# The cache stage of a decoder step in pairs of steps, with part of its transposes moved to VectorE

## The chip, the cores and the metric

One Trainium2 chip, one core of it. The time is that of one execution on the device, in microseconds (us). A core has TensorE (PE, matrix products and transposes), VectorE (DVE), ScalarE (ACT), GpSimd (POOL) and SyncE (SP, here only DMA). Each runs its own list of instructions in order, and they wait for each other by semaphores.

## The reference

One inference step of a decoder layer that has two head groups (a gated delta rule and latent attention) and an MLP, for a prompt of 528 tokens (16 of them meta tokens) and for 8 sample sequences with 4 new tokens each. The part that matters here is the attention of the samples over their past, 4096 keys per sequence. A key is a latent of 256 numbers and a rotary part of 32, and the latent is also the value:

```python
def latent_scores(q_lat, q_pe, c, k_pe):
    s = jnp.einsum('bqhc,bkc->bhqk', q_lat, c) + jnp.einsum('bqhr,bkr->bhqk', q_pe, k_pe)
    return s.astype(jnp.float32) * MLA_SCALE

def sample_attention(q_lat, q_pe, c_new, kpe_new, c_past, kpe_past):
    ...
    p = jax.nn.softmax(jnp.concatenate([s_past, s_new], axis=-1), axis=-1).astype(c_new.dtype)
    return jnp.einsum('bhqk,bkc->bqhc', p[..., :P], c_past) + jnp.einsum('bhqk,bkc->bqhc', p[..., P:], c_new)
```

The past lies in pages of 128 keys, in an order that a page table gives. There are 8 heads, so a sequence has 32 query rows (8 heads by 4 tokens). All of it is fp32.

## The kernel before

The stages follow each other on PE: projections, the gated delta rule, queries and keys, the prompt's attention, then the **cache stage**, then the output product and the MLP (`big_product` and `weight_tile`, lines 589 to 591 of the profile), whose weights SP loads in 1 MB pieces (`load_weights`, L420) and ACT and DVE split into a high and a low part (L1222, L1721).

The cache stage has 16 steps, n = 0 to 15. Steps 0 to 7 belong to sequences 0 to 3 (g = 0), steps 8 to 15 to sequences 4 to 7. In a step each of four sequences b takes 512 keys. POOL fetches them by four indirect DMAs (`gather`, L2328) into `CN[n % 4][b]`, which holds 128 partitions by 4 keys by 288 numbers; there are four such sets. POOL also packs the rotary parts of the four sequences together (`pack_rope`, `KRN`).

The scores need the keys with their 288 numbers along the partitions, so PE transposes them, nine tiles of four 128x128 blocks a step: tiles 0 to 3 the first 128 latents of each sequence, 4 to 7 the other 128, tile 8 the packed rotary parts (`cache_transposes`, L1078). They go into four PSUM banks in turn, and DVE (tiles 0, 2, 4, 6, L2166) and ACT (the others, L1636) copy them to `CT[0]` to `CT[8]`. The score products (`cache_scores`, L1089) give each sequence 32 rows of the output, so four of them lie beside each other on 32 columns of PE each; the rope product (`cache_rope_scores`, L1096) takes all four at once with a query matrix that is zero off its blocks. A step's scores fill one bank, 3 or 4 in turn.

Then comes one softmax step: `cache_max` (L2171 to L2174) reduces 512 scores per row on DVE, takes the running maximum (`ML`) and the difference, `cache_exp` (L1643, L1644) takes the exponential on ACT into `PE_`, `cache_p` (L1104) transposes P on PE, ACT copies it to `PTE` (L1657), `cache_values` (L1113) multiplies it by the latents as they lie in `CN`, and `accumulate` (L2179, L2180) scales and adds on DVE.

The order is written out by hand. On PE, step n's nine transposes are interleaved with the second half of step n-1's scores, the values of step n-2, the first half of step n's scores and P of step n-1, so that what a product needs was issued well ahead of it. ACT and DVE have the same loop. A gather of step n+1 waits for the values of step n-3 (`ce_pv`), since it fills the same buffers.

The stage starts when the prompt's last output is copied (`po_copied`). After it DVE scales the sums (L2193, L2194), PE forms the samples' outputs (L1136, L1143), and the output product starts. Gathers 0 and 1 are made before the stage; 2 and 3 when the prompt's last value product (`pv_done`) is through.

Of the kernel before, what the change touches and what calls it, by code (L numbers as in the profile page):

```python
# [127 lines left out]
def build(nc, big_at, row_at, a):  # L128
# [160 lines left out]
    KRN, PE_, PTE = [], [], []  # L289
    at = r4  # L290
    for i in range(2):
        for name, held, shape in (("KRN", KRN, [P, 4, 4, DR]), ("PE", PE_, [P, 512]), ("PTE", PTE, [P, 4, P])):
            t, at = put(f"{name}{i}", shape, F32, at)
            held.append(t)
    ACC, at = put("ACC", [P, 2, KV], F32, at)
    SME, at = put("SME", [P, 2, 4], F32, at)
# [3 lines left out]
    QF, at = put("QF", [P, 2, 2, P], F32, spec_at)  # L300
    QRF, at = put("QRF", [P, 2, P], F32, at)
    assert at <= r4
    rows_of = 4 * (KV + DR) * 4
    cn_at = [[x + rows_of * b for b in range(4)] for x in (w_at, w_at + 4 * rows_of, x_at + 4 * rows_of, r1)]
# [3 lines left out]
    CT, at = [None] * 9, x_at  # L308
    for i in range(9):
        CT[i], at = put(f"CT{i}", [P, 512], F32, at)  # L310
# [3 lines left out]
    CT_BANKS = (0, 1, 2, 7)  # L314
    CT_DVE = {0: 1, 2: 2, 4: 3, 6: 4}
    CT_ACT = {1: 1, 3: 2, 5: 3, 7: 4, 8: 5}
# [19 lines left out]
    with ctx:  # L336
# [38 lines left out]
        def wait_copied(eng, n, u):  # L375

            if u in CT_DVE:
                eng.wait_ge(sem("ct_dve"), 4 * n + CT_DVE[u])
            else:
                eng.wait_ge(sem("ct_act"), 5 * n + CT_ACT[u])  # L380

        def wait_scored(eng, n, u):

            if n >= 0:
                eng.wait_ge(sem("ct_used"), 3 * n + (1 if u < 4 else 2 if u < 8 else 3))
# [22 lines left out]
        def _(sp):  # L408
# [90 lines left out]
        def _(pe):  # L499
# [444 lines left out]
            def new_transposes(g):  # L944
                pe.wait_ge(sem("new_exp"), g + 1)
                if g:
                    pe.wait_ge(sem("new_acc"), 1)
                pe.transpose(PS[0:NS, 6, 0:P], PE_[0][:, 0:NS], ident).then_inc(sem("new_pt"), 1)

            def new_values(g):  # L950
                pe.wait_ge(sem("new_ptc"), g + 1)
                pe.matmul(PS[:, 6, 0:KV], PTE[0][0:NS, 0, :], CNEW[:, :], start=True, stop=True)                  .then_inc(sem("new_pv"), 1)
# [112 lines left out]
            pe.wait_ge(sem("po_copied"), NT_)  # L1065

            def cache_transposes(n, u):

                x = 9 * n + u
                if x >= 4:  # L1070
                    wait_copied(pe, (x - 4) // 9, (x - 4) % 9)
                if u == 8:
                    pe.wait_ge(sem("kr_packed"), n + 1)
                elif u == 0:
                    pe.wait_ge(sem(f"cn_in{n % 4}"), 64 * (n // 4 + 1))
                for j in range(4):
                    src = CN[n % 4][u % 4][:, j, P * (u // 4):P * (u // 4) + P] if u < 8 else KRN[n % 2][:, j, :, :]
                    last = pe.transpose(PS[:, CT_BANKS[x % 4], P * j:P * j + P], src, ident)  # L1078
                last.then_inc(sem("ct_mm"), 1)

            def cache_scores(n, c):

                if c == 0 and n >= 2:
                    pe.wait_ge(sem("ce_exp"), n - 1)
                g, bank = n // 8, 3 + n % 2
                for b in range(4):
                    wait_copied(pe, n, 4 * c + b)
                for b in range(4):
                    last = pe.matmul(PS[32 * b:32 * b + 32, bank, :], QF[:, g, c, 32 * b:32 * b + 32], CT[4 * c + b][:, :],  # L1089
                                     start=(c == 0), stop=False)  # L1090
                last.then_inc(sem("ct_used"), 1)

            def cache_rope_scores(n):

                wait_copied(pe, n, 8)
                pe.matmul(PS[:, 3 + n % 2, :], QRF[:, n // 8, :], CT[8][:, :], start=False,  # L1096
                          stop=True).then_inc(sem("ct_used"), 1)

            def cache_p(n):
                pe.wait_ge(sem("ce_exp"), n + 1)  # L1100
                if n >= 1:
                    pe.wait_ge(sem("ce_ptc"), n)
                for j in range(4):
                    last = pe.transpose(PS[:, 5, P * j:P * j + P], PE_[n % 2][:, P * j:P * j + P], ident)  # L1104
                last.then_inc(sem("ce_pt"), 1)

            def cache_values(n):
                pe.wait_ge(sem("ce_ptc"), n + 1)
                if n >= 1:
                    pe.wait_ge(sem("acc_done"), n)  # L1110
                for j in range(4):
                    for b in range(4):
                        last = pe.matmul(PS[32 * b:32 * b + 32, 6, 0:KV], PTE[n % 2][:, j, 32 * b:32 * b + 32],  # L1113
                                         CN[n % 4][b][:, j, 0:KV], start=(j == 0), stop=(j == 3))
                last.then_inc(sem("ce_pv"), 1)

            for n in range(18):
                for u in range(9):
                    if n < 16:
                        cache_transposes(n, u)  # L1120
                    if 1 <= n <= 16 and u == 1:
# [1306 lines left out]
```

## Time and profile before

| | |
|---|---|
| Median of 3 runs | 1035.58 us (1034.27 to 1035.91) |
| The profiled execution | 1032.82 us |
| Its span, first to last instruction | 1030.9 us |
| PE busy | 982.4 us, 95% |
| DVE, ACT, POOL busy | 506.8, 445.0, 157.9 us |
| Mean granted clock of TensorE | 0.984 |

Matrix products are pipelined: an instruction that shows 273 ns can start 109 ns after the one before it. So for PE the distance between starts counts, and the chain of waits shows it: each piece of the chain begins where the piece before it ends.

### The profile page before, as it was taken

What the parts mean: (1) busy time and instruction counts of PE and PEld (TensorE: products, weight loads), DVE (VectorE), ACT (ScalarE), POOL (GpSimd) and SP (SyncE); (2) the same over time, 40 slices, a digit from 0 to 9 for tenths busy, and PEclk for the clock granted to TensorE, in tenths of its full rate; (3) what the DMA queues carried; (4) which work ended last, traced back from release to release, by engine and by line L of the source; (5) the groups of instructions that cost most, each with busy time, mean ns of one, the idle gap of its engine ahead of it and who ended that gap; (6) DMA issues with size and microseconds to landing.
All of it is one profiled execution on the core that took longest, in us unless ns stands there. A gap on an engine that the chain in (4) does not pass through costs nothing.

```text
span 1030.9 us, 20604 instructions
## 1 busy us (share of the span) xinstructions
PE 982.4 (95%) x8588; PEld 846.4 (82%) x8588; DVE 506.8 (49%) x992; ACT 445.0 (43%) x963; POOL 157.9 (15%) x257
## 2 busy tenths in 40 slices
PE   4999999999989999899999899999999999999997
PEld 4988899877757556566665799999999999999996
DVE  5665867565475485354444532633343234334423
ACT  5545637566646676344444423431232134113312
POOL 1020500255511201344541000000000000000000
PEclk9999969999999999999999899999999999999999
DMA  7312111220024501577772321422222222222302
GB/s 247 122 46 83 43 42 42 62 48 11 2 68 113 208 1 37 195 238 267 237 241 90 109 83 41 144 82 83 87 102 99 82 83 82 83 86 98 105 1 88
DMA packets 31655, 102.58 MB, mean 100 GB/s; under 512 B 14023, under 2 KB 14967, under 8 KB 25218
## 3 DMA queue, kind: packets, MB, share of 16 engines
q1 hardware_dynamic: 22346, 63.50, 18.7%
q0 software_dynamic: 9216, 37.75, 10.7%
q8 instruction: 69, 1.13, 0.5%
q14 instruction: 24, 0.20, 0.1%
HBM read 96.45 MB, written 4.22 MB: 98 GB/s over the span
## 4 chain that ended last, share of the span: by engine, by line
PE 87%; DVE 6%; ACT 3%; issue 2%; DMA 1%; SPq 0%; DVEq 0%; ACTq 0%
PE PS L589 17%; PE PS L591 17%; PE PS L590 17%; PE PS L1078 7%; PE PS L1089 3%; PE PS L1113 3%; PE PS L724 2%; PE PS L1096 2%; PE PS L797 1%; PE PS L828 1%; PE PS L880 1%; PE PS L979 1%; PE PS L571 1%; DMA RAW<-in_w_stream 1%; PE PS L698 1%
## 5 line engine op out<-in xcount | busy, mean ns | idle before, releaser
L589 PE MATMUL PS<-XH,WH 128*128 128x272 f32 (+1 forms) x928 | 271.4, 292 | 1.8 <-DVE WL L1721 1.8
L591 PE MATMUL PS<-XH,WL 128*128 128x272 f32 (+1 forms) x928 | 270.3, 291 | 0.0
L590 PE MATMUL PS<-XL,WH 128*128 128x272 f32 (+1 forms) x928 | 269.5, 290 | 0.0
L589 PEld LDWEIGHTS PS<-XH,WH 128*128 128x128 f32 x928 | 175.9, 190 | 6.8 <-issue 4.2
L590 PEld LDWEIGHTS PS<-XL,WH 128*128 128x128 f32 x928 | 176.2, 190 | 0.0
L591 PEld LDWEIGHTS PS<-XH,WL 128*128 128x128 f32 x928 | 175.9, 190 | 0.0
L1222 ACT ACTIVATE WH<-RAW 128x2048 fp32r<-128x2048 f32 x46 | 88.0, 1913 | 203.1 <-PE PS L591 203.1
L589 PE MATMUL PS<-NH,WH 128*128 128x272 f32 x512 | 149.1, 291 | 0.8 <-DVE WL L1721 0.8
L591 PE MATMUL PS<-NH,WL 128*128 128x272 f32 x512 | 147.6, 288 | 0.0
L590 PE MATMUL PS<-NL,WH 128*128 128x272 f32 x512 | 146.6, 286 | 0.0
L1721 DVE TENSOR_TENSOR WL<-RAW,WH 128x2048 fp32r<-128x2048 f32 (+1 forms) x48 | 108.1, 2252 | 64.6 <-ACT WH L1222 64.2
L2208 DVE TENSOR_TENSOR HT<-HT,PS 128x272 f32<-128x272 f32 x80 | 31.4, 434 | 137.8 <-PE PS L591 137.8
L589 PEld LDWEIGHTS PS<-NH,WH 128*128 128x128 f32 x512 | 96.3, 188 | 1.3 <-DVE WL L1721 1.0
L590 PEld LDWEIGHTS PS<-NL,WH 128*128 128x128 f32 x512 | 96.1, 188 | 0.3
L591 PEld LDWEIGHTS PS<-NH,WL 128*128 128x128 f32 x512 | 96.2, 188 | 0.0
L2166 DVE COPY CT<-PS 128x512 f32<-128x512 f32 x64 | 44.3, 692 | 87.2 <-PE PS L1078 87.2
L1078 PEld LDWEIGHTS PS<-CST,CN 128*128 128x128 f32 x512 | 58.5, 144 | 29.9 <-issue 15.6
L2328 POOL DMA_INDIRECT CN<-in_cache,IDX x64 | 60.8, 949 | 127.9 <-PE PS L1025 55.2
L1636 ACT ACTIVATE CT<-PS 128x512 f32<-128x512 f32 x80 | 47.3, 597 | 56.7 <-PE PS L1078 55.0
L1078 PE MATMUL PS<-CST,CN 128*128 128x128 f32 x512 | 69.5, 280 | 2.1 <-DVE CT L2166 1.9
L2236 DVE SCALAR_TENSOR_TENSOR AR<-PS,RSTD 128x272 f32<-128x272 f32 x64 | 25.2, 436 | 59.8 <-PE PS L591 59.7
L1686 ACT ACTIVATE AR<-AR 128x544 f32<-128x544 f32 x32 | 20.8, 649 | 61.2 <-DVE AR L2236 61.2
(323 smaller groups left out, 1473.0 us busy)
## 6 DMA issues: line engine op xcount, KB each, us to landing
RAW<-in_w_stream SPq DMA_DIRECT2D x47, 1024.0 KB, 4.8
XN<-in_hin SPq DMA_DIRECT2D x4, 512.0 KB, 6.2
out_y_p<-YO SPq DMA_DIRECT2D x4, 512.0 KB, 2.7
CST<-in_big SPq DMA_DIRECT2D x1, 1132.5 KB, 12.8
SS<-in_sstate SPq DMA_DIRECT2D x1, 1024.0 KB, 5.1
out_ssm_s<-SS SPq DMA_DIRECT2D x4, 256.0 KB
CN<-in_cache,IDX POOLq DMA_INDIRECT x64
WQN<-in_wq SPq DMA_DIRECT2D x3, 256.0 KB, 5.8
```

The costliest lines, as they stand in the source:

```text
L589: pe.matmul(PS[:, b, 0:n], wh, xh[:, k, c:c + n], start=(k == 0), stop=False)
L590: pe.matmul(PS[:, b, 0:n], wh, xl[:, k, c:c + n], start=False, stop=False)
L591: last = pe.matmul(PS[:, b, 0:n], wl, xh[:, k, c:c + n], start=False, stop=(k == DT - 1))
L1078: last = pe.transpose(PS[:, CT_BANKS[x % 4], P * j:P * j + P], src, ident)
L1089: last = pe.matmul(PS[32 * b:32 * b + 32, bank, :], QF[:, g, c, 32 * b:32 * b + 32], CT[4 * c + b][:, :], start=(c == 0), stop=False)
L1113: last = pe.matmul(PS[32 * b:32 * b + 32, 6, 0:KV], PTE[n % 2][:, j, 32 * b:32 * b + 32], CN[n % 4][b][:, j, 0:KV], start=(j == 0), stop=( ...
L1222: act.activation(WH[w % 2][:, :, :], RAW[w % 2][:, :, :], ACT.Copy).then_inc(sem("w_high"), 1)
L1636: act.activation(CT[u][:, :], PS[:, CT_BANKS[(9 * n + u) % 4], :], ACT.Copy).then_inc(sem("ct_act"), 1)
L1721: return dve.tensor_tensor(out, full, high.bitcast(F32), ALU.subtract)
L2166: dve.tensor_copy(CT[u][:, :], PS[:, CT_BANKS[(9 * n + u) % 4], :]).then_inc(sem("ct_dve"), 1)
L2208: last = dve.tensor_tensor(HT[:, j, c:c + n], HT[:, j, c:c + n], PS[:, b, 0:n], ALU.add)
L2328: pool.indirect_dma_start(CN[n % 4][b][:, :, :].rearrange("p r d -> p (r d)"), None, KEYS, bass.IndirectOffsetOnAxis(IDX[:, 4 * n + b:4 * ...
```

## The change

Two steps, 2m and 2m+1, form a pair m, and the stage has 8 pairs.

- Only the first 128 latents of each sequence are transposed by PE (four tiles a step). They go through two banks, 4 and 7, and ACT alone copies them.
- The other 128 latents and the 32 rotary numbers are transposed by DVE from `CN` to `CB`, each 32x32 block in place of its partitions, one instruction for a step and sequence (`block_transpose`, 128 x 640 numbers). So the keys of `CB` lie with 32 numbers on each quarter of the partitions, and quarter q holds the keys of partitions 32q to 32q+31.
- The scores of a pair fill banks 0 to 3: bank q the keys of quarter q, 128 columns for each step. `column_scores` does the first 128 latents, 16 products with 128 columns a step. `block_scores` does the rest once a pair: 5 groups of 32 numbers by 4 quarters by 4 sequences, 80 products with 32 rows and 32 output rows and 256 columns. They need the queries laid out again (`QS`), by 32 small DMAs on SP.
- One maximum, one correction and one accumulation for a pair, two exponentials and two transposes of P. The value products of both steps add into bank 6.
- POOL no longer packs; its gathers wait as before for the values of four steps back.
- The buffers are laid out anew; `CB` is held once, so a pair's blocks can be written only when the scores of the pair before are done.

On PE (shortened):

```diff
-            def cache_transposes(n, u):
-                x = 9 * n + u
-                if x >= 4:
-                    wait_copied(pe, (x - 4) // 9, (x - 4) % 9)
...
+            def cache_transposes(n, b):
+                x = 4 * n + b
+                if x >= 2:
+                    pe.wait_ge(sem("ct_copied"), x - 1)
...
+                    last = pe.transpose(PS[:, 4 + 3 * (x % 2), P * j:P * j + P], CN[n % 4][b][:, j, 0:P], ident)
...
+            def block_scores(m):
+                pe.wait_ge(sem("cb_done"), 8 * m + 8)
+                for x in range(5):
+                    for q in range(4):
+                        rows = slice(32 * q, 32 * q + 32)
+                        for b in range(4):
+                            heads = slice(32 * b, 32 * b + 32)
+                            last = pe.matmul(PS[heads, q, 0:2 * P], QS[rows, m // 4, x, heads],
+                                             CB[b][rows, x, :, :, :].rearrange("p s j k -> p (s j k)"),
+                                             start=False, stop=(x == 4))
                 last.then_inc(sem("ct_used"), 1)
...
+            def column_scores(n):
+                s = n % 2
+                pe.wait_ge(sem("ct_copied"), 4 * n + 4)
+                if s == 0 and n >= 2:
+                    pe.wait_ge(sem("ce_exp"), n)
+                    pe.wait_ge(sem("ce_ptc"), n)
+                for q in range(4):
+                    for b in range(4):
+                        heads = slice(32 * b, 32 * b + 32)
+                        last = pe.matmul(PS[heads, q, P * s:P * s + P], QF[:, n // 8, 0, heads],
+                                         CT[s][b][:, :, 32 * q:32 * q + 32], start=(s == 0), stop=False)
...
+            for m in range(8):
+                column_scores(2 * m + 1)
+                block_scores(m)
+                if m < 7:
+                    step_transposes(2 * m + 2)
+                cache_p(2 * m)
+                cache_p(2 * m + 1)
+                for x in range(8):
+                    cache_values(2 * m + x // 4, x % 4)
+                if m < 7:
+                    column_scores(2 * m + 2)
+                    step_transposes(2 * m + 3)
```

On ACT:

```diff
+            for x in range(8):
+                cache_copy(x // 4, x % 4)
+            for m in range(8):
+                if m < 7:
+                    cache_copy(2 * m + 2, 0)
+                    cache_copy(2 * m + 2, 1)
+                cache_exp(m)
+                cache_copy_p(2 * m)
+                correction(m)
+                cache_copy_p(2 * m + 1)
+                if m < 7:
+                    cache_copy(2 * m + 2, 2)
+                    cache_copy(2 * m + 2, 3)
+                    for b in range(4):
+                        cache_copy(2 * m + 3, b)
```

On DVE:

```diff
+            def block_transpose(n, b):
+                if b == 0:
+                    dve.wait_ge(sem(f"cn_in{n % 4}"), 64 * (n // 4 + 1))
+                    if n >= 2:
+                        dve.wait_ge(sem("ct_used"), 3 * (n // 2 - 1) + 3)
+                dve.transpose(CB[b][:, :, n % 2, :, :].rearrange("p x j k -> p j x k"),
+                              CN[n % 4][b][:, :, P:].rearrange("p j (x c) -> p j x c", c=32)).then_inc(sem("cb_done"), 1)
...
+            for x in range(8):
+                block_transpose(x // 4, x % 4)
+            for m in range(8):
+                cache_max(m)
+                if m < 7:
+                    for x in range(8):
+                        block_transpose(2 * m + 2 + x // 4, x % 4)
+                accumulate(m)
```

On POOL:

```diff
+            for n in range(4, 16):
+                pool.wait_ge(sem("ce_pv"), n - 3)
+                gather(n)
```

On SP:

```diff
+            sp.wait_ge(sem("dve_step"), DVE_STEP["q_padded"])
+            for q in range(4):
+                rows = slice(32 * q, 32 * q + 32)
+                for s in range(4):
+                    src = slice(32 * s, 32 * s + 32)
+                    sp.dma_start(QS[rows, :, s, :], QF[src, :, 1, :]).then_inc(sem("wkbt_in"), 16)
+                    sp.dma_start(QS[rows, :, 4, src], QRF[src, :, src]).then_inc(sem("wkbt_in"), 16)
             sp.wait_ge(sem("ce_pv"), 15)
-            sp.wait_ge(sem("ct_used"), 16 * 3)
+            sp.wait_ge(sem("ct_used"), 3 * 8)
```

## Rows read from the trace of the kernel before

**Rows 1.** The page: engine totals, and the chain that ended last by line.
```profile
PE 982.4 (95%) x8588; PEld 846.4 (82%) x8588; DVE 506.8 (49%) x992; ACT 445.0 (43%) x963; POOL 157.9 (15%) x257
PE PS L589 17%; PE PS L591 17%; PE PS L590 17%; PE PS L1078 7%; PE PS L1089 3%; PE PS L1113 3%; PE PS L724 2%; PE PS L1096 2%; PE PS L797 1%; PE PS L828 1%; PE PS L880 1%; PE PS L979 1%; PE PS L571 1%; DMA RAW<-in_w_stream 1%; PE PS L698 1%
```

**Rows 2.** Stretches: length, busy by engine (PE, PEld, DVE, ACT, POOL), clock, DMA, GB/s.
```profile
404.19:407.60 3.41, 3.13 (x80) 2.84 (x80) 0.00 (x0) 1.13 (x4) 0.00 (x0) 1.00 0.02 5
407.60:411.01 3.41, 3.39 (x16) 3.39 (x17) 1.23 (x2) 0.60 (x1) 2.79 (x3) 0.50 0.46 142
414.43:417.84 3.41, 1.22 (x10) 0.74 (x7) 0.69 (x1) 0.31 (x1) 2.25 (x3) 1.00 0.98 370
417.84:421.25 3.41, 2.98 (x10) 0.83 (x11) 0.69 (x1) 1.38 (x3) 1.00 (x4) 0.50 1.01 418
430.24:554.78 124.54, 124.54 (x1175) 77.29 (x1178) 57.76 (x131) 56.55 (x117) 58.43 (x100) 1.00 0.68 229
```

**Rows 3.** The chain that ended last, one step: start us, us, what.
```profile
430.24 1.86 PE PS L1113 x32
432.11 1.02 PE PS L1078 x8
433.13 1.00 PE PS L1089 x8
434.12 1.46 PE PS L1078 x12
435.59 0.44 PE PS L1104 x4
...
437.89 1.06 PE PS L1096 x2
...
439.82 1.86 PE PS L1113 x32
```

**Rows 4.** Groups by form, 430 to 559 us: busy us, mean ns, then idle time before.
```profile
L2328 POOL DMA_INDIRECT CN<-in_cache,IDX x48 | 45.5, 947 | 66.0 <-PE PS L1113 55.0 <-issue 10.0 <-DMA CN<-in_cache,IDX 0.9
L1636 ACT ACTIVATE CT<-PS 128x512 f32<-128x512 f32 x67 | 39.9, 597 | 43.4 <-PE PS L1078 42.0
L1644 ACT ACTIVATE PE<-PS,SME 128x512 f32<-128x512 f32 x14 | 9.4, 671 | 0.0
L1644 ACT ACTIVATION_READ_ACCUMULATOR PE<-PS,SME 128x1 f32 x14 | 2.7, 191 | 0.0
L2173 DVE TENSOR_TENSOR SME<-SME,ML 128x1 f32<-128x1 f32 x14 | 2.2, 160 | 0.5
```

**Rows 5.** Instructions of PE in order of time, merged: start us, us, line.
```profile
108.12 1.05 PE L628 MATMUL PS<-KQT,KG 128*32 128x32 f32 x96
222.32 0.45 PE L828 MATMUL PS<-VNS,KX 32*128 32x64 f32 x8
396.76 0.60 PE L987 MATMUL PS<-KT,QT 96*32 96x512 f32 x1
396.77 0.18 PE L986 MATMUL PS<-KT,QT 96*32 96x16 f32 x1
```

**Rows 6.** Groups by form of DVE, 340 to 407 us: reductions over 256 and 512.
```profile
L2138 DVE TENSOR_REDUCE SMX<-PS 128x1 f32<-128x512 f32 x8 | 5.5, 691 | 0.3
L2138 DVE TENSOR_REDUCE SMX<-PS 128x1 f32<-128x256 f32 x8 | 3.4, 424 | 0.3
```

**Rows 7.** DMA from 430 to 555 us: packets, MB, share of 16 engines.
```profile
q0 software_dynamic: 6912, 28.31, 67.0%
```

**Rows 8.** Instructions in order of time at the stage's end.
```profile
561.49 1.13 PE L1096 MATMUL PS<-CT,QRF 128*128 128x512 f32 x2
562.65 0.69 DVE L2171 TENSOR_REDUCE SME<-PS 128x1 f32<-128x512 f32 x1 [2.61 <-PE PS L1096]
566.21 1.93 PE L1113 MATMUL PS<-CN,PTE 128*32 128x256 f32 x32 [0.69 <-ACT PTE L1657]
```

**Rows 9.** SP's queue in order of time, its last entry before the stage.
```profile
341.82 0.36 SPq L420 DMA_DIRECT2D RAW<-in_w_stream  x1
```

More of the change, by code:

```diff
@@ L1099, in cache_p @@
             def cache_p(n):
                 pe.wait_ge(sem("ce_exp"), n + 1)
-                if n >= 1:
-                    pe.wait_ge(sem("ce_ptc"), n)
+                if n >= 2:
+                    pe.wait_ge(sem("ce_ptc"), n - 1)
                 for j in range(4):
-                    last = pe.transpose(PS[:, 5, P * j:P * j + P], PE_[n % 2][:, P * j:P * j + P], ident)
+                    last = pe.transpose(PS[:, P_BANKS[n % 2], P * j:P * j + P], PEP[:, 4 * (n % 2) + j, :], ident)
                 last.then_inc(sem("ce_pt"), 1)
[L1107 to L1121, printed above, removed]
-                        cache_scores(n - 1, 1)
-                        cache_rope_scores(n - 1)
-                    if n >= 2 and u == 3:
-                        cache_values(n - 2)
-                    if n < 16 and u == 5:
-                        cache_scores(n, 0)
-                    if 1 <= n <= 16 and u == 8:
-                        cache_p(n - 1)
+            def cache_values(n, j):
+                s = n % 2
+                if j == 0:
+                    pe.wait_ge(sem("ce_ptc"), n + 1)
+                    if s == 0 and n >= 2:
+                        pe.wait_ge(sem("acc_done"), n // 2)
+                for b in range(4):
+                    last = pe.matmul(PS[32 * b:32 * b + 32, 6, 0:KV], PTE[:, 4 * s + j, 32 * b:32 * b + 32],
+                                     CN[n % 4][b][:, j, 0:KV], start=(s == 0 and j == 0), stop=(s == 1 and j == 3))
+                if j == 3:
+                    last.then_inc(sem("ce_pv"), 1)
@@ new lines, in _, with step_transposes @@
+            pe.wait_ge(sem("exp_done"), NS_)
+            pe.wait_ge(sem("wkbt_in"), 16 + 16 * 32)
+            pe.wait_ge(sem("po_copied"), NT_)
+            def step_transposes(n):
+                for b in range(4):
+                    cache_transposes(n, b)
+            step_transposes(0)
+            step_transposes(1)
+            column_scores(0)
+            for m in range(8):
[10 more added lines that the diff above has]
+                    step_transposes(2 * m + 3)
@@ L2179, in accumulate, with cache_max @@
+            def cache_max(m):
+                s = SME[:, m % 3, :]
+                dve.wait_ge(sem("ct_used"), 3 * m + 3)
+                link(dve.tensor_reduce(s[:, 1:2], PS[:, 0:4, 0:2 * P], mybir.AxisListType.XY, ALU.max, negate=True))
+                dve.tensor_tensor(s[:, 1:2], s[:, 1:2], previous_max(m), ALU.min).then_inc(sem("ce_max"), 1)
+            def accumulate(m):
+                g, s = m // 4, SME[:, m % 3, :]
+                dve.wait_ge(sem("ce_pv"), 2 * m + 2)
                 link(dve.scalar_tensor_tensor(ML[:, g, 1:2], ML[:, g, 1:2], s[:, 3:4], s[:, 2:3], ALU.mult, ALU.add))
+                link(dve.tensor_tensor(ML[:, g, 1:2], ML[:, g, 1:2], s[:, 4:5], ALU.add))
@@ L2180, in accumulate @@
                 dve.scalar_tensor_tensor(ACC[:, g, :], ACC[:, g, :], s[:, 3:4], PS[:, 6, 0:KV], ALU.mult,
                                          ALU.add).then_inc(sem("acc_done"), 1)
[L2182 to L2191 removed]
+                dve.wait_ge(sem("acc_done"), m + 1)
@@ L2351, in _ @@
             gather(3)
-            for n in range(2, 16):
-                if n >= 3 and n + 1 < 16:
-                    pool.wait_ge(sem("ce_pv"), n - 2)
-                    gather(n + 1)
-                pack_rope(n)
+            for n in range(4, 16):
+                pool.wait_ge(sem("ce_pv"), n - 3)
+                gather(n)
 def laid_out(x_prompt, x_sample, cache_latent, cache_krope, state_conv, state_ssm, page_table, meta_tokens,
```

163 lines of the change are left out of this document (61 added, 102 removed).

## The prediction

> **What bounds the kernel now.** I read the engine totals first: PE is busy 95% of the span, and the chain of work that ended last is almost all PE [rows 1]. PE's work in the dense products (lines 589 to 591) is not touched; the chain's next entries, L1078, L1089, L1113 and L1096, are the cache stage, and those are what the diff rewrites. It runs from 407.6 us, where the first transpose starts, to the end of the last value product at 568.1 us [rows 2, 8]: 160.5 us for 16 steps. The chain over one step comes next [rows 3]: one value product starts at 430.24, the next at 439.82, so a step takes 9.58 us, and every piece of it is PE. The pieces are 36 transposes (x8, x12 and twice x8: 1.02 + 1.46 and, at 0.44 for four as in the P piece, 2 x 0.87), two latent score products (1.00 each, the second is left out in the rows), the rope product 1.06, four transposes of P 0.44, values 1.86; together 9.58. In the stretch 430.24 to 554.78 PE has no idle time, DVE and ACT are busy 46% and 45%, POOL 47%, DMA 68% [rows 2]. So now only PE's amount of work counts, and any wait that the change makes is paid in full.
>
> **What a PE instruction costs.** Four transposes of 128 columns take 0.44, so one pass over 128 columns is 0.109 us, 0.85 ns a column [rows 3]. A value product is 16 products of 256 columns in two passes, on four column groups at once: 8 rounds of 0.217 = 1.73, and the piece is 1.86, so a change of tile shape costs some 0.13. Two rows show how far small products overlap. L628 issued 96 passes of 32 columns in 1.05 us, 11 ns each. L828 has 32-row operands in four row groups and writes four banks: its 8 passes of 64 columns span 0.45 us, where one behind the other they would need 8 x 0.054 plus latency, 0.7: row groups do run side by side. And a pass of L987 started (396.76) before the last pass of L986 (396.77), which stands ahead of it in the program on another tile: tiles don't wait for each other [rows 5].
>
> **The change on PE, per pair of steps** (before: 19.16 us).
> - Transposes: 32 instead of 72 (block columns 128 to 287 go to DVE): 32 x 0.109 = 3.5.
> - P transposes: 8, 0.87 as before. Values: 32 products in one accumulation, 2 x 1.73 + 0.13 = 3.6.
> - Column scores, twice: 16 products of 128 columns on four tiles, 8 rounds of 0.109 = 0.87, with the shape change 1.0 each: 2.0.
> - Block scores: 80 products with 32 rows and 32 outputs, 256 columns, on 16 tiles. No row shows 16 at once. Low end: 5 products x 2 passes x 0.217 = 2.17, plus 0.2 for two shape changes and the stagger, 2.35. High end, if only column groups overlapped: four times as much, 8.7 + 0.2 = 8.9. I take 2.35, since [rows 5] shows both kinds of overlap and 160 passes at 11 ns (1.8) fit in it.
> The PE work is then 12.3 us a pair, 6.8 less. But the order now has waits.
>
> **The waits.** Only ACT copies the transposes now, 0.60 each, through two banks (4 and 7). A bank's turn is transposes 0.60 with latency, copy 0.60, two semaphores 0.15: 1.35 for two tiles, 0.68 a tile against PE's 0.44. Let T be the end of block_scores(m).
> - DVE: reduce over 1024 elements. The forms of 256 and 512 take 0.424 and 0.691, 1.04 ns an element [rows 6], so 1.22; DVE starts within 0.2 of PE's end [rows 8]; the min 0.16 [rows 4]: max ready at T+1.66.
> - ACT: two copies of the next step's tiles until T+2.0, exp 0.67 + 0.19 read (0.76 with overlap): first P at T+2.76, second at T+3.52. PE transposes P until T+3.25 and T+4.0; ACT copies P from T+3.53 to T+4.13; values run from T+4.2 to T+7.8. PE idles 1.5 here, although four tiles are transposed meanwhile.
> - column_scores(2m+2) to T+8.8, then four tiles of the odd step through two banks: last copy at T+12.05, column_scores(2m+3) T+12.1 to T+13.1. PE idles 1.5 again. block_scores to T+15.5.
> A pair takes 15.5 us instead of 19.16.
>
> **What must stay under cover.** (1) DVE's eight block transposes start at T+1.66 and block_scores(m+1) needs them by T+13.1: 1.43 us each is free. No row shows a DVE transpose. For 640 elements, the slope of [rows 6] gives 0.16 + 640 x 1.04 ns = 0.83; nothing says it can't be below, where it gains nothing. Upper end: four times the slope, 2.8 us. I take 0.83; DVE is done at T+8.3. accumulate stands behind them, and only values(2m+2) waits for it, 4 us later. (2) Gathers: the queue moved 28.3 MB in 12 gathers at 67% of 125 us [rows 7], 7.0 us each at full use, 14 a pair: fits in 15.5, with little left. POOL issues 8 x (0.95 + 0.30) = 10 us [rows 4]; its packing copies go. gather(2m+4) starts at T+6.2, lands by about T+14.5, needed at T+15.5; the next lands 7 later, when DVE wants it 4 us after that T: DVE may wait 1 to 2 us, inside its slack of 4.8. (3) The 32 small DMAs that lay out QS are issued on SP behind the weight load at 341.8 [rows 9]; nothing queues behind them before the stage's end, and even 2 us each would land before 407.6. (4) Softmax sums: one more 0.16 op on DVE, one 0.2 correction on ACT, both beside PE.
>
> **Start and end.** At 407.6 the granted clock is 0.50 until 411.0 [rows 2], from work before the stage, and stays so. Tiles 0 to 3 take 3.7, tiles 4 to 7 2.8 through the two banks, and a last copy ends near 414.5; column_scores(1) to 415.6, first T at 418.0. DVE, idle from 404.2 on [rows 2], has its blocks by 411. Last T: 418.0 + 7 x 15.5 = 526.5. After it no tiles come in between: exp, P, values end 7.6 later, 534.1. What follows (sums scaled, sample outputs, output product) keeps its order and waits for the same last value product. Weights N_IN+1 are requested only 2 us before it, since SP waits for the last block scores and ce_pv 15, but are not wanted until two output tiles are through.
>
> **Sum.** 568.1 - 534.1 = 34.0 us. The profiled execution took 1032.8 us (span 1030.9), the median of the runs 1035.6; I take the difference off the median: 1001.6.
>
> The Trainium skill (TensorE: Matmul & The Clock Gate, Back-to-back issue gap) puts a floor of about 25 ns between matmul starts however small they are. L628's 11 ns disagree here [rows 5], and the measurement decides. By the page the 160 passes would take 4.0 instead of 2.17: 1.8 x 8 more, 1016.
>
> **Rivals.**
> 1. Half overlap: PE holds fewer than 16 tiles in flight, so that a second pass waits for the next row group's first. Then 20 rounds of 0.217 = 4.35, +2.2 x 8 = 17.5 us: 1019. For: no row has 16 tiles. Against: L986/L987. 16%.
> 2. The clock falls inside a pair. In 404.2 to 407.6 PE ran 80 passes of 16 columns and fell to 0.50 next; in 414.4 to 417.8 it was busy 1.2 of 3.4 us and the next stretch again had 0.50 [rows 2]. The new stretches from T to T+4.2 and T+8.8 to T+12.1 hold only transposes, streaming 62% and 54%. Half clock there costs 1.5 to 3 us a pair: 1013 to 1026. Against: in 407.6 to 411.0 PE ran 16 transposes and nothing else, and the clock rose after them [rows 2]. 10%.
> The same page of the Trainium skill (Part 4, PE-mode transpose) says transposes do not count as busy, by which this rival would come true in every pair; the row at 407.60 speaks against it.
> 3. Slower: row groups serialise in block_scores when all four write partitions that the four column groups share (four banks, the same rows). Block scores cost 8.9: +6.55 x 8 = 52 us, 1054. It decides from 2.35 + 34.0/8 = 6.6 us a call. Against: L828 wrote all 128 rows of four banks at once. 7%.
> 4. Slower: DVE's transpose becomes the bound. From 1.43 us each it lengthens the pair, from 1.96 the gain is gone (8 x 0.53 = 4.25 a pair); at 2.8 the pair is 1.66 + 22.4 + 2.35 = 26.4, 1089. 5%.
> 5. The gain is eaten by small waits together with gathers landing late (a pair near 19): about 1030 to 1036. 2%.
>
> **Chances.** Forecast 60% (own range 993 to 1011, by 1 us more or less in a pair). Faster by over 0.2% (2 us, what this measurement can tell from no change) 86%, within it 2%, slower 12%. The range reaches over the half overlap and most of the clock rival: 991 to 1022; below it only if the pair takes under 14.2, which the 14 us of gathers forbid.
>
> **What would show it.** Right: T to T 15 to 16 us; block_scores 2.2 to 2.6 us for its 160 passes; DVE transposes 0.7 to 1.0 us each; in each pair two idle stretches of PE of about 1.5 us, ended by ACT; DMA share near 0.9; clock 1.00 from 411 on. Wrong: block scores of 4 or 9 us, PE waiting for DVE's blocks or for a gather, or a clock row of 0.50 in the stage.

## The result, and the profile after

| | before | after |
|---|---|---|
| Median | 1035.74 us (4 runs, 1034.27 to 1036.28) | 1080.11 us (4 runs, 1078.52 to 1081.63) |
| Ratio | | 1.043, 95% interval 1.041 to 1.045 |
| Span of the profiled execution | 1030.9 us | 1077.8 us |
| Cache stage, first transpose to last value product | 160.5 us | 207.4 us |

The forecast was 1002 us, and it is wrong, in sign too. The whole difference of the spans, 46.9 us, lies in the cache stage. One fact of the experiments belongs here already: in a later session the same two programs took 1028.64 and 1024.68 us, a ratio of 0.995. What sets the two sessions apart is told below.

From the page of the kernel after: engine totals, the row of the granted clock, the shares of the chain that ended last, and the group of ACT's copies. It answers to [rows 1].

```profile
PE 973.3 (90%) x9772; PEld 848.7 (79%) x9772; DVE 500.7 (46%) x936; ACT 431.8 (40%) x939; POOL 141.4 (13%) x193
...
PEclk9999889999999998777777989999999999999999
...
PE 78%; another core or an unknown queue 7%; DVE 6%; ACT 5%; issue 2%; DMA 1%; SPq 0%; ACTq 0%; DVEq 0%
...
L1684 ACT ACTIVATE CT<-PS 128x512 f32<-128x512 f32 x64 | 35.6, 596 | 140.1 <-remote 73.6
```

PE's share has fallen from 95% to 90%, the clock row holds 7s in the stage, and the chain has a releaser that it didn't have before. ACT's copies waited 73.6 us for it. One pair of the chain shows the place (start us, us, what; it answers to [rows 3]):

```profile
453.00 0.60 PE PS L1084 x4
...
455.43 0.67 PE PS L1119 x4
...
457.29 1.08 ACT CT L1684 x2
458.37 12.23 another core or an unknown queue
...
470.62 0.61 ACT CT L1684
...
471.27 1.98 PE PS L1084 x8
...
473.93 1.94 PE PS L1110 x32
475.86 4.43 PE PS L1095 x153
...
480.29 0.60 PE PS L1084 x4
```

A pair takes 27.3 us (453.0 to 480.3), and six of the seven distances between pairs are like that; in the last, for which no key is fetched, it is 16.9. Its first part is as forecast. Then ACT waits 12.2 us for tiles 0 and 1 of the odd step. PE and POOL in the same time (start us, busy us, engine, line, in brackets the idle time before):

```profile
456.78 3.66 PE L1129 MATMUL PS<-CN,PTE 128*32 128x256 f32 x64
460.25 1.26 PE L1110 MATMUL PS<-CT,QF 128*32 128x128 f32 x30
461.82 0.38 PE L1110 MATMUL PS<-CT,QF 128*32 128x128 f32 x2 [0.31 <-issue]
462.13 0.55 PE L1084 MATMUL PS<-CST,CN 128*128 128x128 f32 x3
463.28 0.49 PE L1084 MATMUL PS<-CST,CN 128*128 128x128 f32 x3 [0.60 <-issue]
...
464.75 0.42 PE L1084 MATMUL PS<-CST,CN 128*128 128x128 f32 x1 [0.45 <-issue]
471.27 1.97 PE L1084 MATMUL PS<-CST,CN 128*128 128x128 f32 x8 [6.10 <-ACT CT L1684]
459.01 0.94 POOL L2373 DMA_INDIRECT CN<-in_cache,IDX  x1 [17.64 <-PE PS L1129]
...
467.73 0.94 POOL L2373 DMA_INDIRECT CN<-in_cache,IDX  x1 [0.30 <-issue]
```

The eight transposing passes of two tiles, 0.87 us of work, straggle from 462.13 to 465.2, with "issue" as the reason, and ACT sees the first tile done only at 470.6. The column scores before them end at 462.2, and their semaphore rises at 470.5. That is 1.9 us behind the end of the last of POOL's eight indirect issues (459.01 to 468.67). I call this the hold: PE gets through few instructions, and what it has done is signalled late, while POOL issues indirect transfers. The clock follows (stretch, length, busy PE, PEld, DVE, ACT, POOL, clock, DMA, GB/s):

```profile
451.00:464.70 13.70, 11.83 (x222) 7.75 (x198) 8.09 (x13) 4.67 (x11) 4.47 (x5) 0.99 0.27 90
464.70:478.40 13.70, 6.87 (x125) 4.92 (x139) 0.00 (x0) 2.28 (x4) 3.06 (x4) 0.50 0.70 257
```

So most of what remains of the pair runs at 1.2 GHz: transposes 1.98 instead of 1.15 us, column scores 1.94 instead of 1.08, block scores 4.50 instead of 3.39 (the second figures from nogather_again, below).

### The profile page after: what moved, and what is told of

Read it like the earlier page. It is cut to its first block, busy times and chain, and to the rows that moved or that the text cites. A ratio compares the mean times of both kernels' runs of the same rounds, so it can differ in the third digit from the quotient of the medians.

```text
span 1077.8 us, 22699 instructions
## 1 busy us (share of the span) xinstructions
PE 973.3 (90%) x9772; PEld 848.7 (79%) x9772; DVE 500.7 (46%) x936; ACT 431.8 (40%) x939; POOL 141.4 (13%) x193
## 4 chain that ended last, share of the span: by engine, by line
PE 78%; another core or an unknown queue 7%; DVE 6%; ACT 5%; issue 2%; DMA 1%; SPq 0%; ACTq 0%; DVEq 0%
PE PS L600 16%; PE PS L602 16%; PE PS L601 16%; PE PS L1095 3%; PE PS L1084 3%; PE PS L735 2%; ACT CT L1684 2%; PE PS L1110 2%; PE PS L808 1%; PE PS L839 1%; PE PS L891 1%; PE PS L990 1%; PE PS L582 1%; DMA RAW<-in_w_stream 1%
## 5 line engine op out<-in xcount | busy, mean ns | idle before, releaser
L1684 ACT ACTIVATE CT<-PS 128x512 f32<-128x512 f32 x64 | 35.6, 596 | 140.1 <-remote 73.6
L1084 PE MATMUL PS<-CST,CN 128*128 128x128 f32 x256 | 45.5, 321 | 47.6 <-ACT CT L1684 38.8
L1084 PEld LDWEIGHTS PS<-CST,CN 128*128 128x128 f32 x256 | 33.0, 161 | 59.9 <-ACT CT L1684 43.4
L2217 DVE TENSOR_REDUCE SME<-PS 128x1 f32<-128x1024 f32 x8 | 9.8, 1224 | 132.5 <-PE PS L1095 132.5
L2211 DVE STREAM_TRANSPOSE CB<-CN 128x640 f32<-128x640 f32 x64 | 47.4, 808 | 0.0
```

The lines of the kernel that those rows point to most:

```text
L1084: last = pe.transpose(PS[:, 4 + 3 * (x % 2), P * j:P * j + P], CN[n % 4][b][:, j, 0:P], ident)
L1684: act.activation(CT[n % 2][b][:, :, :], PS[:, 4 + 3 * (b % 2), :].rearrange("p (j k) -> p j k", j=4), ACT.Copy).then_inc(sem("ct_copied"), 1)
L2211: dve.transpose(CB[b][:, :, n % 2, :, :].rearrange("p x j k -> p j x k"), CN[n % 4][b][:, :, P:].rearrange("p j (x c) -> p j x c", c=32)). ...
```

## The experiments

Theories at the start. **A**: POOL's issue of indirect transfers holds PE up. **B**: the bytes that arrive do. **The rival to both**: PE's own order or instruction supply. Each group of experiments ran on one chip in one session, and ratios are to the kernel before on the same chip.

**Four variants of the gathers, on one chip (before: 1033.32 us).**

```diff
 a_nogather: the loop of gathers 4 to 15 removed, the waits on cn_in set to gathers 0 to 3
 a_plain, on SP instead of POOL:
+            for n in range(4, 16):
+                sp.wait_ge(sem("ce_pv"), n - 3)
+                for b in range(4):
+                    sp.dma_start(CN[n % 4][b][:, :, :].rearrange("p r d -> p (r d)"),
+                                 KEYS[P * (4 * n + b):P * (4 * n + b) + P, :]).then_inc(sem(f"x_in{n % 4}"), 16)
 a_smallgather, in the gathers of steps 4 to 15:
-    CN[n % 4][b][:, :, :].rearrange("p r d -> p (r d)"), None, KEYS,
+    CN[n % 4][b][:, 0, 0:32], None, a["cache"].rearrange("a k (x c) -> (a k x) c", c=32),
 a_spread:
+                if n % 2 == 1:
+                    pool.wait_ge(sem("ct_used"), 3 * (n // 2 - 2) + 6)
                 gather(n)
```

> The changed kernel without the gathers of steps 4 to 15 (the steps take the keys of gathers 0 to 3 again, so those scores are of other keys); PE, DVE and ACT run the same instructions. Theory: PE's stall of 12 us in each pair comes from the gathers. Then the stall is gone as in pair 6, where none is issued: a pair takes 16.5 to 17.5 us instead of 27.3, the granted clock stays 1.00, and the time is 1080 - 6 x 10 = about 1015 to 1020. Rival: PE is held up by its own order or instruction supply. Then the pair stays at 27.3 and the time near 1080.

> The changed kernel with the gathers of steps 4 to 15 as plain transfers of the same bytes, issued on SP instead of POOL under the same waits (rows in order and not by the page table). Theory A: what holds PE up is POOL's issue of indirect transfers; then this is like the kernel without gathers, pairs of 16.5 to 18 us and about 1017 to 1025. Theory B: it is the bytes that arrive; then the pair stays near 27 and the time near 1080.

> The changed kernel with the gathers of steps 4 to 15 fetching rows of 128 bytes instead of 4608, with as many indirect issues on POOL (the scores are of other keys). Theory A (POOL's issue holds PE up): the stall lasts as long as before, until about 2 us behind the last of the eight issues, pair 27.3, about 1080. Theory B (the bytes): the stall is gone, pair 16.5 to 18, about 1017 to 1025.

> The changed kernel with the second gather of each pair issued only after the next block scores, so that four issues and not eight stand behind each other. If PE is held up while POOL issues, and the wait costs as much as it lasts beyond what PE has queued, each stall is 5 us shorter but the second gather makes one of its own behind the block scores: pair 18 to 24 us, 1020 to 1055. If the stall hangs on where PE is and not on POOL, it stays 1080.

| | us | ratio, 95% interval | first to last end of block scores / 7 |
|---|---|---|---|
| a_nogather | 1015.79 | 0.983 (0.981 to 0.984) | 16.2 |
| a_plain | 1022.85 | 0.990 (0.989 to 0.992) | 17.4 |
| a_smallgather | 1076.78 | 1.042 (1.041 to 1.044) | 25.3 |
| a_spread | 1047.87 | 1.016 (1.013 to 1.018) | 20.5 |

(The kernel after: 25.8.) The same bytes without POOL cost nothing of the stall; POOL's issues with hardly a byte cost all of it. a_smallgather, first the gathers' row of the DMA from 430 to 555 us (packets, MB, share of 16 engines; [rows 7] had 28.31 MB and 67%), then a piece of its chain:

```profile
q0 software_dynamic: 1280, 0.66, 3.1%
```

```profile
430.45 12.14 another core or an unknown queue
```

As causes of the stall B and the rival fall, and A stands: here it is the issuing. All four times came as expected. In a_spread, with four issues behind each other and not eight, no piece of the chain has the unknown releaser any more; it waits for keys that are asked for late, 6.7 us of transfer where PE has nothing else:

```profile
452.37 6.71 DMA CN<-in_cache,IDX
```

**Other ways to fetch, and the block scores, on a second chip (before: 1028.96 us).**

```diff
 a_pages and b_pages (the same in the kernel before), on SP:
+                    _, v = nc.values_load_multi_w_load_instructions(PG[0:1, 16 * n + 4 * b:16 * n + 4 * b + 4], ...)
+                    for j in range(4):
+                        sp.dma_start(CN[n % 4][b][32 * j:32 * j + 32, :, :]..., a["cache"][bass.ds(v[j], 1), :, :]...)
 a_gap, on POOL for each m:
+                pool.wait_ge(sem("ce_pv"), 2 * m + 1);      gather(2 * m + 4, (0, 1))
+                pool.wait_ge(sem("ct_used"), 3 * m + 4);    gather(2 * m + 4, (2, 3))
+                pool.wait_ge(sem("ct_copied"), 8 * m + 14); gather(2 * m + 5, (0, 1))
+                pool.wait_ge(sem("ct_used"), 3 * m + 5);    gather(2 * m + 5, (2,))
+                pool.wait_ge(sem("ct_used"), 3 * m + 6);    gather(2 * m + 5, (3,))
 a_half, in block_scores of a_nogather:
-    PS[heads, q, 0:2 * P], ..., CB[b][rows, x, :, :, :].rearrange("p s j k -> p (s j k)"),
+    PS[heads, q, 0:P], ..., CB[b][rows, x, 0, :, :].rearrange("p j k -> p (j k)"),
```

> The whole of the changed kernel, with the keys of steps 4 to 15 fetched on SP page by page: SP reads four page numbers of the table into registers and issues four transfers of 128 keys for a step and sequence. If POOL's indirect issues are what the change collides with, this is like the run with plain transfers, 1021 to 1028, if SP's reads and 32 issues per pair take less than the 17 us of a pair; if they take longer (over 0.5 us for one of the 32), the pair waits for its keys and the time is 1030 to 1060.

> The kernel before, with its keys of steps 4 to 15 fetched on SP page by page in the same way. Its PE had no idle time in the stage although its increments came up to 2.2 us late, so by my reading the hold was covered: within 3 us of before. Rival: POOL's issues slowed PE's own work there as well; then it is faster by 5 us or more, and the change would gain less against it.

> The changed kernel with its eight indirect issues of a pair in five groups of 2, 2, 2, 1 and 1, each behind another step of PE or ACT. If PE's increments are held until the last of a run of issues is through, each run now holds them 1 to 2.5 us: pair 18 to 21 us and about 1025 to 1045. If it is the number of issues that costs and not how they stand, the stall is as long in sum: 1070 to 1080.

> The changed kernel without the gathers of steps 4 to 15, and its block products with 128 columns instead of 256 (those of the odd step are left out, so its scores lack 160 of 288 numbers); as many instructions. It runs against a_nogather, where the 160 passes took 3.3 to 4 us. Theory: what limits 32x32 products is the rate at which PE issues instructions. Then they take as long as with 256 columns, 3.3 us or more. Rival (half of the tiles overlap, so that streaming counts): 10 rounds less, about 1.7 to 2.2 us, and the time is 1.6 x 8 = 13 us below a_nogather.

Measured: a_pages 1042.91 us, 1.014 (1.012 to 1.015); b_pages 1036.34, 1.007 (1.006 to 1.008); a_gap 1021.71, 0.993 (0.992 to 0.995); a_half 1004.46, 0.976 (0.975 to 0.978). Of the expectations only that of a_pages came in, by its second half: it is bound by SP. b_pages was expected within 3 us of before and is 7.4 above, with PE waiting 5.3 us for keys that SP asks for late. a_gap is below both of its ranges. a_half is 11.3 us below a_nogather, where 13 were expected, but 4.4 of them lie between the kernels before on the two chips; beside nogather_again (0.981, below) it gains 0.5%. In the chain of a_pages a read of page numbers (0.30) and four issues at 0.50 follow each other without a pause, 2.32 us for a step and sequence, 18.6 a pair:

```profile
486.77 0.32 SPq L502
...
487.12 0.30 SPq L498
...
487.59 0.32 SPq L502
```

a_gap looked like the cure: no stall, though seven of its eight issues stand nearly back to back. From this I made **theory D**: a wait of POOL between issues frees PE. It was tested next, with the waits one at a time. (The changed kernel itself hadn't run on this chip, so neither its stall nor a cure was shown there.)

**The waits one by one, on a third chip (before: 1028.47 us).**

```diff
 a_four:
+                pool.wait_ge(sem("ce_pv"), n - 3)
+                gather(n)
+                pool.wait_ge(sem("ct_used"), 3 * (n // 2 - 2) + 4)
+                gather(n + 1)
 a_waits, in gather, ahead of each issue but the first:
+                    if n >= 4 and b:
+                        pool.wait_ge(sem("ce_pv"), n - 3)
 a_late8:
+                pool.wait_ge(sem("ct_used"), 3 * (n // 2 - 2) + 4)
+                gather(n)
+                gather(n + 1)
 a_gap2: a_gap with its last two waits on ct_copied 8 * m + 16 and ct_used 3 * m + 5
```

> The changed kernel, and the second gather of a pair waits for the column scores behind the values (ct_used) instead of for the values themselves, some 1 us later; the eight issues still stand back to back. In a_gap, where seven issues stood nearly back to back but with such waits between them, PE wasn't held up. If a wait on another event between the issues is what frees PE, the stall is gone or halved: 1020 to 1050. If what matters is that the issues are few or apart, it stays: 1070 to 1080.

> The changed kernel, in which each indirect issue of a gather repeats its wait (ce_pv, long satisfied). If a wait instruction between issues, satisfied or not, frees PE, the time is 1020 to 1030. If not, 1075 to 1085.

> The changed kernel with its eight issues of a pair in one run without any wait between them, which starts behind the column scores (1.2 us after the values are through) and not in the middle of the values. If a run of eight holds PE up wherever it stands, the pair is 27 us or more and the time 1075 to 1090. If the hold hangs on what PE does when the run starts, it is less, and the time is 1020 to 1050.

> The kernel a_gap with its last issues of a pair earlier: the seventh behind a copy of ACT and the eighth behind the column scores of the odd step, not behind the block scores. If short groups with waits between them are enough, a gather lands earlier and the time is 1 to 5 us below a_gap's; if the length of the whole run counts, the stall comes back: 1040 to 1080.

Measured: a_four 1023.04 us, 0.995; a_waits 1023.55, 0.995; a_gap2 1022.35, 0.994 (each with an interval of 0.002 on either side; a_gap2 isn't below a_gap, as its expectation had it); a_late8 1038.33, 1.010 (1.008 to 1.011). That every variant was cured alike, even the one that only repeats a satisfied wait, was suspicious. And the run of eight issues at the stage's start, which all kernels have unchanged, no longer disturbed PE either. The suspicion: not the waits, but where and when they ran. a_late8 has no stall; its keys come late, pairs of 20.5.

**The same kernels on one chip (a fourth, before: 1028.64 us).**

> The changed kernel itself, unchanged, once more. The last eight kernels ran on chips where the kernel before takes 1028 to 1029 us and not 1033 to 1036, and there the run of eight issues at the stage's start, the same in all kernels, no longer slowed PE. Theory C: the hold is a property of the chip and not of the order of POOL's waits; on a chip where the kernel before takes 1029 this kernel takes 1020 to 1027, on one where it takes 1034 it takes 1080. Theory D (the waits between the issues decide): 1075 to 1085 on any chip.

> The kernel a_waits once more (the changed kernel with each indirect issue repeating its wait), beside the changed kernel on the same chip. Theory C: the same time as the changed kernel, whatever that is. Theory D: 1020 to 1027 whatever the chip.

> The kernel a_nogather once more, on the same chip as the changed kernel. If this chip holds PE up during POOL's issues, the changed kernel is 60 us or more above this; if it doesn't, only late keys are between them, 5 to 12 us, and this is at 1010 to 1015.

> The kernel before without its gathers of steps 4 to 15 (these steps take the keys of gathers 0 to 3 again, so those scores are of other keys). PE had no idle time in its stage, so without gathers it should be the same within 2 us; if POOL's issues cost the kernel before something too (the 6 us between chips), it is 4 to 8 us faster on a chip that holds PE up.

| | us | ratio, 95% interval |
|---|---|---|
| after_again | 1024.68 | 0.995 (0.993 to 0.997) |
| waits_again | 1020.88 | 0.994 (0.992 to 0.996) |
| nogather_again | 1009.97 | 0.981 (0.979 to 0.983) |
| b_nogather | 1028.50 | 1.000 (0.999 to 1.001) |

Theory D falls as the account of these runs: the unaltered changed kernel has no stall here. Theory C fits all runs, but a state that passed fits them too: the two sessions with the hold (the result and the first four experiments) are also the two earliest of six, and the chip of the experiments with the hold was not seen again. So whether the hold comes is a matter of the chip or of its state at the time; the program alone doesn't decide it. One expectation was missed: nogather_again is 14.7 us below after_again, not 5 to 12. The stage's start shows the hold with the same instructions, first the kernel after on the chip of the result, then after_again:

```profile
413.36 1.28 PE L1110 MATMUL PS<-CT,QF 128*32 128x128 f32 x32
...
415.65 0.41 PE L1110 MATMUL PS<-CT,QF 128*32 128x128 f32 x4 [0.44 <-issue]
415.85 0.94 POOL L2373 DMA_INDIRECT CN<-in_cache,IDX  x1 [0.30 <-issue]
417.08 0.37 PE L1110 MATMUL PS<-CT,QF 128*32 128x128 f32 x1 [1.02 <-issue]
417.79 2.25 PE L1110 MATMUL PS<-CT,QF 128*32 128x128 f32 x26 [0.34 <-issue]
```

```profile
414.34 1.95 PE L1110 MATMUL PS<-CT,QF 128*32 128x128 f32 x64
415.36 0.94 POOL L2373 DMA_INDIRECT CN<-in_cache,IDX  x1 [0.31 <-issue]
```

POOL's issues take 0.94 us on both. PE is held up in the session of the result and in that of the first four experiments (which chip the result is from isn't known); in the four later ones, on three other chips than that of the first four experiments, it isn't. So A is shown where the hold is, and elsewhere it doesn't apply. Of the variants that alter the order of POOL's issues only a_spread ran with the hold, and there two groups of four had no stall of 12 us. Whether shorter groups or waits between the issues help there stays open: those variants ran without the hold. So does what causes it.

**An order that hides ACT's copies, and the kernel before, on the fourth chip again (before: 1028.15 us).**

```diff
 a_order, on PE:
                 for x in range(8):
+                    if m < 7 and x in (4, 6):
+                        cache_transposes(2 * m + 3, x - 4)
+                        cache_transposes(2 * m + 3, x - 3)
                     cache_values(2 * m + x // 4, x % 4)
                 if m < 7:
                     column_scores(2 * m + 2)
-                    step_transposes(2 * m + 3)
```

> The changed kernel with PE's order altered: tiles 0 and 1 of the odd step's transposes stand between the two halves of the pair's values, tiles 2 and 3 before its last quarter, so that their copies by ACT run beside the values. In after_again PE waits 0.25 + 0.69 us a pair for these copies. If PE's order sets the pair, it is 0.7 us shorter, 5 us in all: 0.990 of the kernel before on a chip that doesn't hold PE up. If late keys set it (14 us of gathers in a pair of 17 to 19), nothing is gained: 0.994 to 0.996. On a chip that holds PE up it is at 1.03 to 1.05 like the changed kernel.

> The kernel before, unchanged, for its trace on this chip. If the chip is one of those that don't hold PE up (1027 to 1030 us), its stage is 156 to 157 us long, as in b_nogather, instead of 160.5, and no increment of PE is late; if it is one of the others (1033 to 1036 us), 160 to 161.

a_order took 1021.23 us, 0.9926 (0.9908 to 0.9943), beside 0.9951 for the kernel after: the best median ratio of the versions that compute all, though its interval overlaps those of a_gap (0.9918 to 0.9947), waits_again and, by a little, the kernel after (0.9931 to 0.9971). It lies between the two expectations (0.990, and 0.994 to 0.996), so the gain isn't clear of the noise. Its waits for ACT's copies fell from 7.3 us to 0.7, and 2.9 us of that came back as waits for keys (1.7 us in after_again, 4.6 here). Waits of PE in a_order:

```profile
PE PS L1095 <- issue: 9.4, 5, 2.8
PE PS L1084 <- DMA CN<-in_cache,IDX: 4.6, 4, 1.9
```

before_again took 1027.74 us, and its stage 155.9 us instead of 160.5. The pieces at the stage's start, of the kernel before on the chip of the result and then of before_again:

```profile
413.09 2.98 PE PS L1078 x16
...
416.09 0.70 DVE CT L2166
...
417.50 0.78 issue
```

```profile
412.21 2.33 PE PS L1078 x20
414.54 0.99 PE PS L1089 x8
```

The hold was in the trace of before already: DVE's copy waited for a tile until 416.09, one "issue" piece of 0.78 followed, and the clock fell. It cost the kernel before 4.6 us of the stage, all of them ahead of the first value product. After that it went on, under cover. One row of the trace of before, 430 to 559 us, shows it:

```profile
L1657 ACT ACTIVATE PTE<-PS 128x512 f32<-128x512 f32 x13 | 7.8, 598 | 16.3 <-remote 16.1 <-PE PS L1104 0.2
```

ACT's copy of P waited 16.1 us for a releaser that the profile doesn't know, though the program runs on one core. In most steps it starts 2.1 to 2.2 us behind the end of the P transposes; in before_again 0.13 us behind them, and no such releaser is left. PE had other work in the meantime, so it cost nothing.

## Why the prediction was wrong

The ledger, in us of the stage. Forecast: 126.5 (407.6 to 534.1).

| | stage | more than the line above |
|---|---|---|
| forecast | 126.5 | |
| without gathers (nogather_again) | 138.3 | 11.8 |
| with gathers, no hold (after_again) | 153.2 | 14.9 |
| with the hold (the kernel after) | 207.4 | 54.2 |

**The step that failed** is number (2) of what must stay under cover: "POOL issues 8 x (0.95 + 0.30) = 10 us", against a pair of 15.5. I priced the issues as POOL's time and the gathers as bytes, and nothing as a cost to PE. In the session of the result it is PE's: ACT's wait for tiles 0 and 1 is 12.25 us a pair instead of 3.57 (after_again and nogather_again), 8.7 more; the half clock behind it costs 0.8 in transposes, 0.9 in column scores and 1.1 in block scores; that is the whole 11.5 between 27.3 and the 15.8 of an undisturbed pair. The kernel before has 4 issues at a time and four banks of tiles copied by two engines, and PE had no idle time in it; the changed one has 8 at a time, two banks and one engine, and stands still. Which of these differences decides wasn't separated, but for a_spread, which has 4 at a time. That the trace gave warning is the lesson: [rows 2] show PE busy 1.22 of 3.41 us at 414.43 while POOL issued (in before_again, 413.85 to 417.26, it is 3.41 of 3.41), and I took it for a question of the clock only (rival 2) and never asked what PE waited for; and the unknown releaser of L1657 stood in the trace. Rival 5 came nearest in kind, and none of mine held a pair of 27 us by way of PE itself.

**Point by point, without the hold.**

*Waits and order: right in kind, the sum partly by luck.* An undisturbed pair takes 15.8 us (nogather_again, 440.9 to 456.7; three more like it); 15.5 was forecast. The waits behind ACT's two banks are there, 0.25 and 0.69, and a turn of the banks takes 1.35 as forecast (tiles 0 and 2 are copied from 449.79 and 451.14). Values run from T+3.8 to T+7.4, forecast T+4.2 to T+7.8, and the block scores start 0.7 earlier than forecast. That offsets most of what they are too long themselves.

*Block scores: mis-sized by 1.0.* They were put at 2.35 and measured 3.39 at full clock. First the kernel a_nogather with 256 columns, then a_half with 128:

```profile
458.43 3.39 PE L1095 MATMUL PS<-CB,QS 32*32 32x256 f32 x160
```

```profile
482.25 2.32 PE L1095 MATMUL PS<-CB,QS 32*32 32x128 f32 x160
```

Half of the columns takes 1.07 us away. Ten rounds of passes of 128 columns less are 10 x 0.109 = 1.09 [rows 3]: all 16 tiles do stream side by side. Rival 1 would have given 2.2 and rival 3 far more, and both are excluded. So is the theory that only the number of passes counts. What was missing is, by the straight line through these two widths, a fixed part of 1.25 us for 160 passes where I had 0.2; the term is 8 x 1.04 = 8.3 us in all. The rule of the Trainium skill that the prediction weighed (TensorE: Matmul & The Clock Gate, Back-to-back issue gap) gives, by its 25 ns a pass, an estimate of 4.0 us for either, and the runs disagree: 160 passes in 2.32 us are 14.5 ns each.

*DVE: right.* Eight transposes take 5.93 us, 0.81 by the mean of a group (forecast 0.83), and the reduction 1.22 (forecast 1.22). From the kernel after:

```profile
L2211 DVE STREAM_TRANSPOSE CB<-CN 128x640 f32<-128x640 f32 x60 | 44.5, 808 | 0.0
L2217 DVE TENSOR_REDUCE SME<-PS 128x1 f32<-128x1024 f32 x8 | 9.8, 1224 | 132.5 <-PE PS L1095 132.5
```

*Start: short by 4.9.* First T at 15.3 us into the stage and not 10.4 (nogather_again), 1.0 for the block scores, 2.3 for a gap inside them (below), the rest mostly at half clock behind it. With 5.5 in seven distances and 1.5 at the end this makes the 11.8 (but for rounding).

*Gathers without the hold: 14.9, forecast nothing.* Pairs take 16.9 to 21.4 us in after_again. Here is what PE waited for, first after_again, then nogather_again (us in total, times, longest):

```profile
PE PS L1095 <- issue: 10.3, 5, 3.6
PE PS L1084 <- DMA CN<-in_cache,IDX: 1.7, 3, 0.6
```

```profile
PE PS L1095 <- issue: 2.9, 3, 2.3
```

PE's waits for late keys are short. Half of the 14.9 is in gaps inside the block scores, released by nothing that the profile shows; some 3 more are in the transposes behind them, which take up to 3.6 us a step instead of 2.5. Where the gaps occur they stand at the same passes in every variant (after pass 120 in pair 0, 99 in pair 2, 152 in pair 3, 130 in pair 5), in a_plain too, where POOL issues nothing in the last three of these pairs; and in the longest one the DMA's instruction queue moves 16 KB beside a gather that fills the engines. The end of that gap in after_again, and the DMA over it, 476.52 to 480.11:

```profile
480.11 1.07 PE L1095 MATMUL PS<-CB,QS 32*32 32x256 f32 x8 [3.60 <-issue]
```

```profile
q0 software_dynamic: 349, 1.43, 99.3%
q8 instruction: 1, 0.02, 1.7%
```

I read these gaps as PE running out of instructions: it uses its program up in the 160 passes faster than the next piece comes. The traces say so in two ways. The 16 traces of the changed kernel and its variants have 57 gaps of over 0.45 us between the starts of two block score passes, up to 4.0 us long, and every one ends 1.2 to 1.6 us after a 16 KB transfer of the instruction queue has landed; with one such transfer in some 7 us, chance would put one gap in 20 there. And shorter passes don't help: a_half is through its first 152 passes of pair 3 sooner and goes on no sooner, 3.72 us from the first pass to pass 153, against 3.76 in nogather_again. First a_half, then nogather_again:

```profile
465.69 2.25 PE L1095 MATMUL PS<-CB,QS 32*32 32x128 f32 x152
469.41 0.42 PE L1095 MATMUL PS<-CB,QS 32*32 32x128 f32 x8 [1.46 <-issue]
```

```profile
469.10 3.32 PE L1095 MATMUL PS<-CB,QS 32*32 32x256 f32 x152
472.86 0.63 PE L1095 MATMUL PS<-CB,QS 32*32 32x256 f32 x8 [0.43 <-issue]
```

Still, no run here changed the supply alone. What the gathers do to it is their bytes: in pairs 2, 3 and 5 the gaps, from start to start, are 9.2 us in after_again, 6.9 in a_plain and 0.8 in nogather_again. So theory B, wrong for the stall, holds for this smaller loss. The Trainium skill (Runtime: NRT & Kernel Launch, Instruction fetch mechanics) says the fetch is mostly hidden because instructions are dispatched more slowly than they are filled in; if the reading is right, this case is an exception of up to 3.6 us. In after_again a stretch of granted clock 0.50 also begins at the end of each gap of over 2 us (from 459.2 to 462.6 behind the one at 456.4): the transposes there took 3.3 us with their wait for ACT, at full clock 2.5. So rival 2 came true in part, by another cause.

The chances were off too, with 86% on faster. Without the hold the sign is the forecast one, by 0.5% and not 3.3%, so the range would have been missed there as well (1024.68 against 993 to 1011).

## What to carry to other kernels

Software-issued gathers are work that other engines may pay for. Before an order with few banks and long waits takes the place of one with slack, look at what every engine does while POOL issues them, and count a stretch in which PE is half idle with "issue" as its reason, or a wait with an unknown releaser in a program of one core, as a warning and not as noise. Small products that fill 16 tiles stream fully in parallel, but have a fixed cost (here 1.25 us for 160 passes) and may empty the instruction supply; to spread them among longer ones may help (not tested). And when a cure works in every variant, run the unaltered kernel again on the same chip before believing it.

## What was not expected of the hardware

- In two of six sessions PE was slowed down while POOL issued indirect transfers, in the others it wasn't; with transfers of 128 bytes a row as much as with 4608 (stall of 12.14 and 12.23 us). This program took 55 us more (1080.1 against 1024.7), the one before 7 (1035.7 against 1028.6), of which its stage shows 4.6. POOL's own 0.94 us an issue was the same in all.
- PE can pause in the middle of a dense run of small passes with nothing to wait for in the profile, up to 3.6 us, and goes on 1.2 to 1.6 us after a 16 KB transfer of the instruction queue has landed.
- Sixteen 32x32 tiles work at once: 160 passes of 128 columns in 2.32 us, of 256 in 3.39.
- SP issues a transfer whose address is in a register every 0.50 us (a_pages), too slow for 32 a pair.
